# Conv's last two tap pairs behind the next chunk's rotated q, and turns of the identity at the MLP's borders

## The chip, the cores and the metric

The kernel runs on one core of a Trainium2 chip. The metric is the time of one execution on the device, in microseconds (us). Five engines work side by side, each through its own queue in order: TensorE (PE, with its weight loads as PEld), VectorE (DVE), ScalarE (ACT), GpSimd (POOL) and SyncE (SP, which here issues the weight loads from memory). They wait for each other through semaphores.

## The reference

Two blocks run one after the other on x of 256 tokens by 2048 features, float32. The change lies in the first one:

```python
h = rmsnorm(x, norm_mix_pre)
xr, yr, q, k, v, g_rnn, g_attn = split(h @ w_in)
xr = causal_depthwise_conv(xr, conv_w, conv_b)      # 4 taps
xr = rg_lru(xr, ...)
y_rnn = xr * gelu(yr)
q, k = rope(q), rope(k)
y_att = sliding_window_sink_attention(q, k, v, sinks)   # 32 q heads, 4 kv heads, blocks of 128
mix = sigmoid(g_rnn) * (y_rnn @ w_rnn_proj) + sigmoid(g_attn) * (y_att @ w_attn_proj)
x = x + rmsnorm(mix @ w_out)
h = rmsnorm(x, norm_mlp_pre)
x = x + rmsnorm(square(relu(h @ w_mlp_up)) @ w_mlp_down)
```

The second block is a differential attention beside an S5 state space branch, again between a norm and projections.

## The kernel before

**Units and steps.** All large products are cut into units: one unit makes 512 output columns for all 256 tokens from up to 2048 inputs. A unit has 8 steps (4 in the short ones); a step takes one weight tile `raw` of 256 by 512 that SP has loaded. ACT copies it to `w_hi` (rounded to fp32r, L660), DVE subtracts to get `w_lo` (L1149, two inputs in SBUF), and TensorE multiplies the high and low halves of both operands, three matmuls for each block (L1847 to L1850 where the result is laid out by feature, L1855 to L1857 where by token). The four-deep ring lets ACT and DVE run three steps ahead: the function `steps` on each engine splits tile j + 3 and then runs the hooks of place j. Hooks are other work, put between the splits or between the matmuls at places that are written out by hand.

**The stage of q and xr.** First comes a unit for k and v and one for the first 512 columns of q. Then for each of four chunks c a unit of xr and a unit of the next chunk's q follow (three times in a loop; the fourth time the second unit is yr). Beside the two units of chunk c its attention runs, eight heads in four pairs p:

- the rotated q of the chunk, staged in `stg`, is turned (L1870) after the second step of the xr unit; ACT copies it out, and the scores of pair 0 are made (L1926) after the third step, of pair 1 after the fifth
- `soft(p)` on DVE scales the scores and adds the mask (L1326, which frees the score bank for the next pair), then takes the maxima; for pair 0 it stands behind the fourth `w_lo` of the unit
- ACT's exponentials (L775 to L778), DVE's totals (L1338, L1339), and POOL's `normalise` (L499, two instructions)
- TensorE turns the probabilities (L1937), ACT copies them (L784), and TensorE multiplies by v (L1944)

At the end of the q unit DVE's `rotate_q` reads the product and writes the rotated q to `stg`, four instructions for each half of the tokens: two that read PSUM (L1279, L1280) and two that read `tmp` and `tmp2` in SBUF (L1282, L1283). The last one counts up `stg_ready`, for which the turn of the next chunk waits. DVE then goes on with the next three `w_lo`.

**POOL in this stage** has one queue: for each chunk the normalising of pairs 0 and 1, the first tap of conv (L513), the normalising of pairs 2 and 3, and then three pairs of conv instructions, each a multiply to `tap` (L518) and an add (L520) over 4 x 256 elements in each partition. `conv(c, 0)` counts up `conv_ready`, for which DVE waits before it writes the next chunk's xr over conv's input.

**The borders of the MLP.** Before the MLP and behind it, x gets a normed residual. TensorE has ended its last unit; ACT sums squares, DVE forms the mean square, POOL takes the root, and DVE's `residual(c)` (L1517) writes the new x, quarter by quarter. `turn_x(c)` (L1885) waits for each quarter (`x_new`) and turns it in two halves; ACT's `x_high` (L708) and DVE's `x_low` (L1198) copy it out to `h_hi` and `h_lo`; the first unit behind the border begins when quarter 0 is copied. The banks `side[0]` and `side[1]` take the odd quarters. No wait of another engine stands on `side[1]` between the last unit and the first turn into it.

Of the kernel before, what the change touches and what calls it, by code (L numbers as in the profile page):

```python
# [16 lines left out]
P = 128  # L17
# [15 lines left out]
NH = D // NC  # L33
# [61 lines left out]
def griffin_block_then_ssm_block(nc, a, inv_freq, out):  # L95
    with ExitStack() as ctx:
        def sb(name, shape, dt=F32):
            return ctx.enter_context(nc.sbuf_tensor(name, shape, dt))
# [10 lines left out]
        def sem(name):  # L109
            return ctx.enter_context(nc.semaphore(name))  # L110
# [19 lines left out]
        ident = sb("ident", [P, P])  # L130
# [32 lines left out]
        side = [sides[:, n * NC:(n + 1) * NC] for n in range(2)]  # L163
# [9 lines left out]
        stg_ready, tps_ready, tps_hi = sem("stg_ready"), sem("tps_ready"), sem("tps_hi")  # L173
# [102 lines left out]
        T_K, T_QX = NH, NH + 1  # L276
# [54 lines left out]
        def lin(i, stride, const):  # L331
            return const if i is None else i * stride + const
# [101 lines left out]
        def _(pool):  # L434
# [47 lines left out]
            for n in range(5):  # L482
                pool.wait_ge(ms_ready, n + 1)
                pool.tensor_tensor(small[:, 6:8], small[:, 4:6], neg_half[:, 0:2], ALU.pow).then_inc(rstd_ready, 1)
                if n == 0:

                    def load_rg(c):
                        for g, name in enumerate(("w_rg_a", "w_rg_x")):
                            for b in range(2):
                                pool.dma_start(rgw[c % 2][g][:, 2 * b:2 * b + 2, :],  # L490
                                               a[name][0][2 * c + b].rearrange("(k p) c -> p k c", p=P))\
                                    .then_inc(rgw_landed[c % 2], 16)

                    def normalise(i, c, p):

                        pool.wait_ge(total_ready, lin(i, 4, 4 * c + p + 1))
                        for t, at in ((0, slice(0, P)), (1, slice(P, 3 * P))):
                            r_ = att[:, 2 * p:2 * p + 2, 10 + t:11 + t].broadcast_to([P, 2, at.stop - at.start])
                            ins = pool.tensor_tensor(prob[p][:, :, at], prob[p][:, :, at], r_, ALU.mult)  # L499
                            if t == 0:  # L500
                                chain.mark(ins)
                        ins.then_inc(norm_ready, 1)

                    def conv(c, k):


                        late = 3 - k
                        if k == 3:
                            for m in range(QPC):
                                at = c * QPC + m  # L510
                                w = pt1[:, COL1["conv_w"] + KT * k + at:COL1["conv_w"] + KT * k + at + 1]
                                b = pt1[:, COL1["conv_b"] + at:COL1["conv_b"] + at + 1]
                                chain.mark(pool.tensor_scalar(slab_d[:, at, :], xr_c[:, m, :], w, b, ALU.mult, ALU.add))  # L513
                            chain.wait()
                            return
                        at = COL1["conv_w"] + KT * k + c * QPC
                        w = pt1[:, at:at + QPC].unsqueeze(2).broadcast_to([P, QPC, SEQ - late])
                        chain.link(pool.tensor_tensor(tap[:, :, late:], xr_c[:, :, 0:SEQ - late], w, ALU.mult))  # L518
                        o = slab_d[:, c * QPC:(c + 1) * QPC, late:]
                        ins = pool.tensor_tensor(o, o, tap[:, :, late:], ALU.add)  # L520
                        if k:
                            chain.link(ins)
                        else:
                            ins.then_inc(conv_ready, 1)

                    load_rg(0)
                    pool.wait_ge(tps_ready, NH)
                    load_rg(1)

                    pool.sem_inc(conv_ready, 1)  # L530
                    for c in range(NH):
                        normalise(None, c, 0)
                        normalise(None, c, 1)
                        pool.wait_ge(acc_free[0], c + 2)
                        conv(c, 3)
                        normalise(None, c, 2)
                        normalise(None, c, 3)
                        conv(c, 2)
                        conv(c, 1)
                        conv(c, 0)  # L540
                    for c in range(2, NH):
                        pool.wait_ge(rg_done, c - 1)
                        load_rg(c)
                    pool.wait_ge(pe_used, U_OUT * S)
                    pool.dma_start(slab_i[:, :, :].rearrange("p (t k) c -> p t (k c)", t=TT),
                                   a["x"][0].rearrange("(t p) d -> p t d", p=P)).then_inc(post_landed, 16)
                    pool.dma_start(slab_f[:, 0:8, :].rearrange("p k c -> p (k c)"),
                                   a["norm_mix_post"].broadcast_to([P, D])).then_inc(post_landed, 16)
                    pool.dma_start(slab_f[:, 8:16, :].rearrange("p k c -> p (k c)"),
                                   a["norm_mlp_post"].broadcast_to([P, D])).then_inc(post_landed, 16)  # L550
                    for n_, name in enumerate(("ssm_b_re_2", "ssm_b_im_2")):
                        pool.dma_start(b_raw[:, n_], a[name][0].rearrange("(t h) p c -> (h p) t c", h=2)).then_inc(b_landed, 16)
                    for n_, name in enumerate(("ssm_c_re_2", "ssm_c_im_2")):
                        pool.dma_start(c_raw[:, n_], a[name][0].rearrange("(m g) c p -> (g c) m p", g=8)).then_inc(b_landed, 16)
                    chain.link(pool.iota(keep[:, 1, :].bitcast(I32), [[1, SEQ]], base=0, channel_multiplier=0))
                    pool.tensor_copy(keep[:, 0, :], keep[:, 1, :].bitcast(I32)).then_inc(t_ready, 1)
# [55 lines left out]
        def x_bank(c, b):  # L612

            if c % 2 == 0:
                return tps[:, b * SEQ:(b + 1) * SEQ]
            return side[b // 2][:, b % 2 * SEQ:(b % 2 + 1) * SEQ]

        SCORES_AT = [5, 9, 15, 19]
        SOFT_AT = [k // 2 + 1 for k in SCORES_AT]
        TURN_P_AT = [13, 18, 23, 28]
# [1200 lines left out]
        def _(pe):  # L1824
            T = nc.tensor
# [37 lines left out]
            def turn(i, stride, t_index, blocks=QPC):  # L1863
# [7 lines left out]
                                          ident[:, :])  # L1871
                ins.then_inc(tps_ready, 1)

            def turn_x(c, t0, first_x):

                if first_x is None:
                    pe.wait_ge(x_landed[c], 16)
                else:
                    pe.wait_ge(x_new, first_x + c + 1)
                if t0 or c >= 2:  # L1880
                    pe.wait_ge(tps_free, t0 + max(c - 1, 0))
                for half, done in enumerate((x_half, tps_ready)):
                    for t in range(TT):
                        for b in (2 * half, 2 * half + 1):
                            ins = T.transpose(x_bank(c, b)[:, t * P:(t + 1) * P],  # L1885
                                              x_tok[:, t, c * NC + b * P:c * NC + (b + 1) * P], ident[:, :])
                    ins.then_inc(done, 1)
# [23 lines left out]
            for c in range(2):  # L1911
                turn_x(c, 0, None)
# [4 lines left out]
            def attention(i, c):  # L1917
# [12 lines left out]
                def turn_p(p):  # L1930
                    pe.wait_ge(norm_ready, lin(i, 4, 4 * c + p + 1))
                    if p:
                        pe.wait_ge(att_out, lin(i, 4, 4 * c + p))
                    for n in range(2):
                        for b in range(3):
                            at = slice(b * P, (b + 1) * P)
                            ins = T.transpose(turned_p[:, n, at], prob[p][:, n, at], ident[:, :])  # L1937
                    ins.then_inc(pt_done, 1)
# [10 lines left out]
                for p, at in enumerate(SOFT_AT):  # L1949
                    places += [(SCORES_AT[p], lambda p=p: scores(p)), (TURN_P_AT[p], lambda p=p: turn_p(p)),  # L1950
                               (TURN_P_AT[p] + 2, lambda p=p: by_v(p))]
# [46 lines left out]
            for c in range(NH):  # L1998

                unit(None, 0, (U_OUT + c) * S, 0, U_OUT + c, slab_dr, slab_gr,  # L2000
                     hooks={5: [lambda: turn(None, 0, T_MIX + NH - 1)]} if c == 0 else None,
                     before={6: [lambda: pe.wait_ge(tps_free, T_MIX + NH)]} if c == 0 else None)
            for c in range(2):
                turn_x(c, T_MLP_IN, 0)

# [10 lines left out]
            with pe.Fori(0, NH - 1) as f:  # L2016
                mlp_units(f, 1)

            for c in range(2):
                turn_x(c, T_N2, NH)  # L2020

# [166 lines left out]
```

## Time and profile before

| | |
|---|---|
| Median of 3 runs | 2317.41 us (2316.6 to 2319.15) |
| The profiled execution | 2315.3 us |
| Its span, first to last instruction | 2313.6 us |
| Mean granted TensorE clock | 0.996 of full |
| PE busy | 2252.5 us |
| DVE, ACT, POOL busy | 1429.7, 1197.5, 383.3 us |

An engine's busy time is the time covered by its instructions; an instruction that another one holds up in memory counts as busy for as long as it takes. The time that an engine sits idle shows in a timeline in square brackets, with the engine and line that released it. A timeline merges like instructions that follow each other into one row: the first number is its start, the second the time from the start of the first to the end of the last, and xN says how many they are.

### The profile page before, as it was taken

The numbers are of one execution on the slowest core, as the hardware profiler recorded it, in microseconds if no ns is written. First come the engines' busy times: TensorE is split into PE (matmuls) and PEld (weight loads), VectorE is DVE, ScalarE is ACT, GpSimd is POOL, SyncE is SP. The second block draws the span as 40 slices with busy tenths as digits, with TensorE's granted clock in tenths as the row PEclk, the third lists the DMA queues.
The fourth block names the chain that finished last, engine by engine and source line by source line (L and its number), as shares of the span: only waits on it lengthen the run. The fifth ranks groups of instructions, "written<-read, shape, count | busy, mean of one in ns | idle before, by whom it ended". The sixth has DMA issues, their size and how long they took to land.

```text
span 2313.6 us, 32956 instructions
## 1 busy us (share of the span) xinstructions
PE 2252.5 (97%) x11754; PEld 1893.6 (82%) x11754; DVE 1429.7 (62%) x1625; ACT 1197.5 (52%) x1851; POOL 383.3 (17%) x408
## 2 busy tenths in 40 slices
PE   7999999999999999999999999998999999999999
PEld 6888899788888778888888888888977778888887
DVE  6666657644554575555555555566799977675554
ACT  5555557544444446555555555555444445554442
POOL 2133440000000102212122121211243311110000
PEclk9999999999999999999999999999999999999999
DMA  8544454566666846666666666665566655556655
GB/s 246 166 140 138 140 151 149 174 190 192 190 190 193 262 157 199 201 204 205 196 204 201 194 208 201 197 206 171 178 177 182 186 172 170 164 164 188 187 189 163
DMA packets 215027, 427.01 MB, mean 185 GB/s; under 512 B 14032, under 2 KB 14320, under 8 KB 214384
## 3 DMA queue, kind: packets, MB, share of 16 engines
q1 hardware_dynamic: 206720, 398.51, 56.3%
q0 software_dynamic: 7744, 26.62, 3.6%
q8 instruction: 83, 1.36, 0.2%
q14 instruction: 48, 0.39, 0.0%
q10 hardware_dynamic: 432, 0.13, 0.0%
HBM read 414.71 MB, written 10.49 MB: 184 GB/s over the span
## 4 chain that ended last, share of the span: by engine, by line
PE 82%; DVE 9%; ACT 3%; issue 3%; DMA 2%; POOL 1%; SPq 0%; ACTq 0%; DVEq 0%
PE acc L1855 23%; PE acc L1857 23%; PE acc L1856 22%; PE acc L1847 3%; PE acc L1849 3%; PE acc L1850 3%; DVE w_lo L1149 3%; PE tps L1870 1%; DMA raw<-in_w_out_dram 1%; ACT w_hi L660 1%; DMA raw<-in_w_in_dram 1%; PE tps L1976 1%; PE sides L1976 1%; PE sides L1926 1%; POOL tmp L577 1%
## 5 line engine op out<-in xcount | busy, mean ns | idle before, releaser
L1149 DVE TENSOR_TENSOR w_lo<-raw,w_hi 128x1024 fp32r<-128x1024 f32 x752 | 938.7, 1252 | 769.1 <-ACT w_hi L660 764.4
L660 ACT ACTIVATE w_hi<-raw 128x1024 fp32r<-128x1024 f32 x752 | 794.4, 1059 | 905.6 <-PE acc L1857 746.1
L1855 PE MATMUL acc<-w_hi,h_hi 128*128 128x512 f32 x1440 | 572.8, 398 | 6.9 <-DVE w_lo L1149 5.8
L1857 PE MATMUL acc<-w_hi,h_lo 128*128 128x512 f32 x1440 | 562.8, 391 | 0.0
L1856 PE MATMUL acc<-w_lo,h_hi 128*128 128x512 f32 x1440 | 561.9, 390 | 0.0
L1855 PEld LDWEIGHTS acc<-w_hi,h_hi 128*128 128x128 f32 x1440 | 271.2, 188 | 75.0 <-issue 15.8
L1857 PEld LDWEIGHTS acc<-w_hi,h_lo 128*128 128x128 f32 x1440 | 271.0, 188 | 57.8
L1856 PEld LDWEIGHTS acc<-w_lo,h_hi 128*128 128x128 f32 x1440 | 271.4, 188 | 53.2
L1855 PE MATMUL acc<-w_hi,slab_dg_r 128*128 128x512 f32 x768 | 300.1, 391 | 3.9 <-DVE w_lo L1149 3.9
L1857 PE MATMUL acc<-w_hi,slab_dg_r 128*128 128x512 f32 x768 | 299.3, 390 | 0.0
L1856 PE MATMUL acc<-w_lo,slab_dg_r 128*128 128x512 f32 x768 | 299.3, 390 | 0.0
L1847 PE MATMUL acc<-h_hi,w_hi 128*128 128x256 f32 x768 | 222.0, 289 | 3.1 <-DVE w_lo L1149 2.8
L1849 PE MATMUL acc<-h_lo,w_hi 128*128 128x256 f32 x768 | 217.9, 284 | 0.0
L1850 PE MATMUL acc<-h_hi,w_lo 128*128 128x256 f32 x768 | 217.8, 284 | 0.0
L1855 PEld LDWEIGHTS acc<-w_hi,slab_dg_r 128*128 128x128 f32 x768 | 144.6, 188 | 34.2 <-issue 4.3
L1857 PEld LDWEIGHTS acc<-w_hi,slab_dg_r 128*128 128x128 f32 x768 | 144.4, 188 | 30.0
L1856 PEld LDWEIGHTS acc<-w_lo,slab_dg_r 128*128 128x128 f32 x768 | 144.6, 188 | 29.8
L1847 PEld LDWEIGHTS acc<-h_hi,w_hi 128*128 128x128 f32 x768 | 147.5, 192 | 9.7 <-issue 5.8
L1849 PEld LDWEIGHTS acc<-h_lo,w_hi 128*128 128x128 f32 x768 | 147.7, 192 | 0.2
L1850 PEld LDWEIGHTS acc<-h_hi,w_lo 128*128 128x128 f32 x768 | 147.7, 192 | 0.0
L1855 PE MATMUL acc<-w_hi,slab_f_r 128*128 128x512 f32 x256 | 100.4, 392 | 0.0
L1857 PE MATMUL acc<-w_hi,slab_h_r 128*128 128x512 f32 x256 | 99.7, 389 | 0.0
(371 smaller groups left out, 2315.1 us busy)
## 6 DMA issues: line engine op xcount, KB each, us to landing
raw<-in_w_in_dram SPq DMA_DIRECT2D x328, 512.0 KB, 3.8
raw<-in_w_mlp_up_dram SPq DMA_DIRECT2D x128, 512.0 KB, 3.8
raw<-in_w_mlp_down_dram SPq DMA_DIRECT2D x128, 512.0 KB, 4.7
raw<-in_w_out_dram SPq DMA_DIRECT2D x64, 512.0 KB, 4.6
raw<-in_w_rnn_proj_dram SPq DMA_DIRECT2D x32, 512.0 KB, 4.4
raw<-in_w_attn_proj_dram SPq DMA_DIRECT2D x32, 512.0 KB, 3.9
trig_scratch<-tmp POOLq DMA_DIRECT2D x32, 256.0 KB, 4.3
raw<-in_w_proj_ssm_dram SPq DMA_DIRECT2D x16, 512.0 KB, 3.8
```

The costliest lines, as they stand in the source:

```text
L577: pool.tensor_tensor(t1[:, 0, :], t1[:, 0, :], t2[:, 1, :], ALU.add).then_inc(mixed_ready, 1)
L660: nc.scalar.activation(w_hi[:, j % RING], raw[:, j % RING], ACT.Copy).then_inc(hi_ready, 1)
L1149: V.tensor_tensor(w_lo[:, j % RING], raw[:, j % RING], w_hi[:, j % RING].bitcast(F32), ALU.subtract)\
L1847: T.matmul(o, wh[:, c], hi[:, k, :], start=first and m % 2 == 0, stop=False, skip_group_check=True)
L1849: T.matmul(o, wh[:, c], lo[:, k, :], start=False, stop=False, skip_group_check=True)
L1850: ins = T.matmul(o, wl[:, c], hi[:, k, :], start=False, stop=last, skip_group_check=True)
L1855: T.matmul(o, hi[:, k, c], wh, start=first, stop=False)
L1856: T.matmul(o, hi[:, k, c], wl, start=False, stop=False)
L1857: ins = T.matmul(o, lo[:, k, c], wh, start=False, stop=last)
L1870: ins = T.transpose(tps[:, b * SEQ + t * P:b * SEQ + (t + 1) * P], stg[:, t, b * P:(b + 1) * P], ident[:, :])
L1926: ins = T.matmul(side[n][:, t * P:t * P + (t + 1) * P], q_c[at, p, t * P:(t + 1) * P], k_c[at, 0:(t + 1) * P], start=True, stop=True)
L1976: ins = T.matmul(bank[:, m * SEQ:(m + 1) * SEQ], rgw[c % 2][g][:, 2 * b + k, m * P:(m + 1) * P], slab_d[:, c * QPC + 2 * b + k, :], start= ...
```

## The change

In POOL's queue a wait is put between the second and the third tap of conv, for chunks 0 to 2: the last two multiply and add pairs, four instructions, begin only when DVE has announced the rotated q of the next chunk. On TensorE a function `keep_turning` is added that transposes the identity into the four quarters of `side[1]`, which nobody reads; it is called 32 times ahead of the first `turn_x` before the MLP and 44 times ahead of the first behind it.

```diff
                         conv(c, 2)
+                        if c < NH - 1:
+                            pool.wait_ge(stg_ready, T_QX + c + 2)
                         conv(c, 1)
                         conv(c, 0)
...
+        WARM = [32, 44]
...
+            def keep_turning(times):
+
+                for n in range(times):
+                    T.transpose(side[1][:, n % 4 * P:(n % 4 + 1) * P], ident[:, :], ident[:, :])
...
+            keep_turning(WARM[0])
             for c in range(2):
                 turn_x(c, T_MLP_IN, 0)
...
             with pe.Fori(0, NH - 1) as f:
                 mlp_units(f, 1)
 
+            keep_turning(WARM[1])
             for c in range(2):
                 turn_x(c, T_N2, NH)
```

## Rows read from the trace of the kernel before

**Rows 1.** The page: busy time and share of the span, each engine.

```profile
PE 2252.5 (97%) x11754; PEld 1893.6 (82%) x11754; DVE 1429.7 (62%) x1625; ACT 1197.5 (52%) x1851; POOL 383.3 (17%) x408
```

**Rows 2.** Timeline of PE, stage of q: start, duration, what, idle before.

```profile
130.32 1.09 PE L1870 MATMUL tps<-ident,stg 128*128 128x128 f32 x8 [2.47 <-DVE stg L1283]
...
141.01 0.93 PE L1926 MATMUL sides<-k_c,slab_dg_f 64*128 64x128 f32 x8
...
147.73 0.81 PE L1937 MATMUL tps<-ident,slab_i_f 128*128 128x128 f32 x6
...
151.35 0.88 PE L1944 MATMUL tps<-slab_e_f,pi 128*64 128x128 f32 x12
...
189.61 1.09 PE L1870 MATMUL tps<-ident,stg 128*128 128x128 f32 x8 [2.47 <-DVE stg L1283]
...
250.30 1.09 PE L1870 MATMUL tps<-ident,stg 128*128 128x128 f32 x8 [2.39 <-DVE stg L1283]
```

**Rows 3.** Timeline of DVE: rotation without conv (66.89), and a chunk later.

```profile
66.89 0.42 DVE L1282 TENSOR_TENSOR stg<-tmp 128x256 f32<-128x256 f32 x1
...
116.07 1.43 DVE L1149 TENSOR_TENSOR w_lo<-raw,w_hi 128x1024 fp32r<-128x1024 f32 x1 [2.06 <-ACT w_hi L660]
...
123.45 1.90 DVE L1282 TENSOR_TENSOR stg<-tmp 128x256 f32<-128x256 f32 x1
125.27 2.10 DVE L1283 TENSOR_TENSOR stg<-tmp 128x256 f32<-128x256 f32 x1
...
128.60 1.25 DVE L1282 TENSOR_TENSOR stg<-tmp 128x256 f32<-128x256 f32 x1
...
130.87 3.50 DVE L1149 TENSOR_TENSOR w_lo<-raw,w_hi 128x1024 fp32r<-128x1024 f32 x3 [0.68 <-DVE stg L1283]
...
136.55 0.95 DVE L1326 SCALAR_TENSOR_TENSOR slab_i_f<-sides,mask 128x768 f32<-128x768 f32 x1
```

**Rows 4.** Timeline of POOL, the same chunk.

```profile
114.54 1.89 POOL L518 TENSOR_TENSOR slab_e_f<-slab_dg_f,pt 128x1020 f32<-128x1020 f32 x1
...
122.67 2.39 POOL L520 TENSOR_TENSOR slab_dg_f<-slab_dg_f,slab_e_f 128x1016 f32<-128x1016 f32 x1
125.14 1.94 POOL L518 TENSOR_TENSOR slab_e_f<-slab_dg_f,pt 128x1012 f32<-128x1012 f32 x1
...
144.00 1.62 POOL L499 TENSOR_TENSOR slab_i_f<-slab_i_f,att 128x256 f32<-128x256 f32 x2 [14.43 <-DVE att L1339]
```

**Rows 5.** Timeline of DVE, a place in the S5 stage.

```profile
1711.05 1.58 DVE L1149 TENSOR_TENSOR w_lo<-raw,w_hi 128x1024 fp32r<-128x1024 f32 x1
1712.55 1.23 DVE L1640 TENSOR_TENSOR_SCAN k_t<-s5p,k_t 128x256 f32<-128x256 f32 x1
```

**Rows 6.** Timeline of POOL at the same place.

```profile
1711.51 1.73 POOL L578 TENSOR_TENSOR k_t<-k_t 128x256 f32<-128x256 f32 x1
```

**Rows 7.** Timeline of ACT: the first exponential of pair 0, the copy L784.

```profile
139.21 0.28 ACT L775 ACTIVATE att<-att,sinks 128x2 f32<-128x2 f32 x1
...
149.40 0.79 ACT L784 ACTIVATE slab_e_f<-tps 128x768 f32<-128x768 f32 x1
```

**Rows 8.** Windows of 1 us: length, busy each engine, clock, DMA.

```profile
192.00:193.00 1.00, 1.00 (x7) 1.00 (x6) 1.00 (x2) 0.36 (x1) 0.00 (x0) 0.50 0.60 59
...
859.00:860.00 1.00, 1.00 (x6) 0.85 (x5) 1.00 (x4) 0.99 (x4) 0.00 (x0) 0.50 0.00 0
860.00:861.00 1.00, 0.77 (x5) 0.50 (x4) 1.00 (x3) 1.00 (x4) 0.00 (x0) 0.99 0.03 8
```

**Rows 9.** Timeline of PE at the borders: first turns of x.

```profile
856.58 1.97 PE L1885 MATMUL tps<-ident,slab_i_f 128*128 128x128 f32 x8 [4.30 <-DVE slab_i_f L1517]
...
863.29 1.04 PE L1885 MATMUL tps<-ident,slab_i_f 128*128 128x128 f32 x8
...
1580.41 1.97 PE L1885 MATMUL tps<-ident,slab_i_f 128*128 128x128 f32 x8 [5.47 <-DVE slab_i_f L1517]
```

**Rows 10.** Timeline of DVE at the first border: `x_low` of quarter 0.

```profile
858.61 1.73 DVE L1198 SCALAR_TENSOR_TENSOR h_lo<-tps,pt,h_hi 128x256 fp32r<-128x256 f32 x4 [0.76 <-ACT h_hi L708]
```

## The prediction

> **What bounds the kernel now.** I read the page first: TensorE is busy for 97% of the span [rows 1], so time comes only out of its idle stretches, of its clock, or out of new idle put into it. The view of waits over the whole span then names who ends its idle time; two entries belong to this change, the turn of the rotated q (L1870) and the first turn of x at the two borders of the MLP (L1885). The timelines give their places. Three turns of the rotated q find TensorE idle for 2.47, 2.47 and 2.39 us [rows 2], 7.33 us in all; the borders find it idle for 4.30 and 5.47 us [rows 9].
>
> **Why the rotated q is late.** Rotating one chunk takes VectorE eight instructions. In the chunk without conv beside it, the one that reads two SBUF tiles and writes half of stg takes 0.42 us; one chunk later its like take 1.90, 2.10 and 1.25 us [rows 3]. Put against the POOL rows [rows 4] these are waits: the one issued at 123.45 ends 0.29 us after conv's add ends (122.67 + 2.39 = 125.06), the one issued at 125.27 ends 0.29 us after conv's next multiply (125.14 + 1.94 = 127.08). So an instruction of VectorE with two SBUF inputs isn't slowed in proportion, it is held until the running POOL instruction ends. The w_lo subtraction behaves alike: issued at 116.07, it ends at 117.50, 1.07 us after the multiply issued at 114.54 ends at 116.43. The holding goes in turns. In the later S5 stage w_lo is issued at 1711.05, a POOL add at 1711.51, and VectorE's scan at 1712.55, when w_lo is all but done; the POOL add ends first (1713.24) and the scan only at 1713.78 [rows 5, 6]. VectorE doesn't keep the access because its next instruction stands ready: whoever asked first has it. The Trainium skill says that GpSimd shares its SBUF interfaces with VectorE and collides with instructions of two SBUF inputs (GPSIMD Engine Reference, Key points). The rows agree, and add the turns. By the page alone, conv beside w_lo would be no cheaper than conv beside the rotation.
>
> **Part 1, removed.** Conv's last four POOL instructions leave the rotation. Its end moves from 130.19 (0.13 before the turn at 130.32) by 1.48 + 1.68 + 0.83 = 3.99 us to 126.2. TensorE comes to the turn at 130.32 - 2.47 = 127.85, 1.65 us later. The three waits, 7.33 us, go.
>
> The clock comes with it. After the second turn TensorE is granted half speed (1.2 of 2.4 GHz) for a few us [rows 8]; the distance from the first turn to the second is 59.29 us and from the second to the third 60.69 us with nearly the same gap in each [rows 2]. That fall cost 1.4 us. It followed one of three equal gaps, so I count it as gone, with 0 and 2.8 as the other ends.
>
> **Part 1, moved.** The four instructions now begin when the rotated q is announced, 126.3. What stands there is w_lo: three subtractions back to back after the rotation (130.87, 3.50 us [rows 3]), then a fourth, then the softmax's first instruction for the next chunk (the scaling at 136.55). VectorE gets to its first w_lo 0.68 us after the rotation (130.87 against 130.19), POOL needs about 0.1 us after a releaser, so POOL goes first, and then they alternate: multiply, w_lo, add, w_lo, multiply, w_lo, add, w_lo. POOL takes 1.89 + 2.39 + 1.89 + 2.39 = 8.56 us, w_lo 4 x 1.07 = 4.28 us: the fourth w_lo ends at 139.1 and the scaling begins at about 139.0. Without any gap and without conv it would begin at 136.55 - 2.47 = 134.1. It is 4.9 us late. The w_lo tiles themselves are in time: the first two end at 129.3 and 132.7, and the two steps that need them lie before the second scores of 138.5, about 3 us each, so they start at about 132.5 and 135.5.
>
> What waits for the scaling, each place as today's row less 2.47 us:
> - The second scores' matmuls (141.01, so 138.54) need the score bank read. It is read at 139.0 + 0.95, seen at 140.05: TensorE waits 1.5 us.
> - The exponentials (ACT, 139.21 [rows 7]) have some 0.3 us to spare now, so they come 4.6 us late. Behind them in ACT's queue stands the next w_hi, behind that w_lo, the totals, and POOL's normalise (144.00, 1.61 us [rows 4]), each right behind the other. Normalise ends at 145.61 - 2.47 + 4.6 = 147.7; TensorE's turn of the probabilities (147.73, so 145.26) goes at 147.8. It is then 2.6 us behind in all.
> - The copy of the turned probabilities (149.40, 0.79 us [rows 7]) ends at 150.19 - 2.47 + 4.6 = 152.3; the product with v (151.35, so 148.88) goes at 152.4: 3.5 us behind in all. After this ACT and VectorE have idle stretches, and I find no further wait in that chunk.
>
> So each of three chunks gives up a wait of 2.4 to 2.5 us and takes up 3.5 us in three smaller ones: 10.5 - 7.33 = +3.2 us. The new wait delays nothing else: POOL's conv ends at about 138, its next work is that normalise, and the copy of xr that overwrites conv's input comes after it. No DMA is moved. The ends: if w_lo were never held, the three new waits would be zero (-7.3); the full holding is the sum above, and waits could grow by 0.3 each if a POOL instruction took longer.
>
> **Part 2, the borders.** 32 and 44 turns of ident into side[1] (unread; its next writer is TensorE itself) are added ahead of the first turn of x. Eight turns at the full clock take 1.04 us [rows 9]: 0.13 us each at most, since the drain of the last one is in it; without it I estimate 0.10. That makes 3.2 to 4.2 us in a gap of 4.30, and 4.4 to 5.7 us in one of 5.47. I take the lower figure, since spacing and not the drain of the last one counts in a row; they are then hidden, the cover being the norm's sums, its root and the residual. At the upper figure the second border loses 0.2 us. What they can give is the clock: the eight turns after the gap take 1.97 us at half speed against 1.04. Only the first four stand before ACT's copy that releases the first h_lo, 0.47 us, and VectorE stood idle for 0.76 us before it [rows 10], so all 0.47 us carries through. Two borders: -0.9 us. The lower end is nothing; the upper end is the clock falling later, on matmuls in place of turns, 1.4 us each.
>
> The Trainium skill has a rule against this part (TensorE: Matmul & The Clock Gate, Part 4): work in transpose mode doesn't count as busy for the clock. The trace disagrees: from 856.58 to 860.2 TensorE ran transposes alone, and the grant went from 0.50 to 0.99 behind them [rows 8]. By that rule the borders would give nothing, and the sum would be 0.9 us higher.
>
> **Sum.** +3.2 - 1.4 - 0.9 = +0.9 us. The profiled execution took 2315.3 us, 1.7 more than its span of 2313.6 and 2.1 less than the median of the three runs, 2317.41. So 2316.2 for such an execution, 2318.3 for the median of runs. A measurement of this kernel can tell about 0.2%, 4.6 us; this is no change.
>
> **Rivals.**
> - *The gap goes and nothing replaces it.* w_lo gets through beside conv at 1.4 us each, as the row at 116.07 has it; then the scaling is no later than 135.5, scores and exponentials are in time, and the whole 7.3 + 1.4 + 0.9 = 9.6 us is gained: 2307.8. For it: w_lo's single instructions beside conv cost little. Against it: those stood alone, with idle time on both sides, and here four stand in a row against four. 22%.
> - *w_lo gets in first.* The alternation begins with VectorE; without the last add in front of it the fourth w_lo ends 2 us sooner, the scaling is 2.9 us late, the second scores don't wait, and behind the exponentials (2.6 us late in place of 4.6) 1.5 us are left of the 3.5: 3 x 1.5 - 7.33 - 1.4 - 0.9 = -5.1, 2312.3. Against it: POOL's 0.1 us against VectorE's 0.68. 12%.
> - *Slower: the clock falls on the scattered waits.* In place of one gap every chunk has waits of 1.5, 1.1 and 0.9 us within 14 us. Today one of three gaps of 2.4 us brought half speed, at 1.4 us. If it fell once in each of three chunks: +0.9 + 3 x 1.4 = +5.1, 2322.5. It decides from the third fall. Against it: each wait is shorter than the gap that brought it once in three. 12%.
> - *The spare turns outlast their gaps.* If they ran at half speed throughout (1.97 us for eight, some 0.22 each), 32 and 44 take 7.0 and 9.7 us, 6.9 us too long. Against it: they follow matmuls at the full clock. Under 3%, within the slower share.
>
> **How the numbers follow.** The forecast has about half, and the rest lies mostly below it. Faster by over 0.2% (under 2312.8) takes the first rival and a good half of the second: 0.29. Slower by over 0.2% (over 2322.0): 0.13. Within: 0.58. The range goes from the first rival to the third, 2307.8 to 2322.5; the likeliest case alone would be 2316 to 2321.
>
> **What would show it.** In the changed profile the three waits of L1870 for stg are gone, and the rotation takes 4.1 us in each chunk. TensorE's waits have new entries: scores (L1926) for the scaling (L1326), turns (L1937) for normalise (L499) and the product with v (L1944) for ACT's copy (L784), three of each and some 10 us together. The w_lo rows behind the rotation read 2.4 to 3.6 us. At the borders the grant stays at full, x's first eight turns take about 1.1 us, and the unit starts 0.5 us sooner. If w_lo there reads 1.4 us and L1926 doesn't wait, the first rival holds. The prediction is wrong if the turns at the port aren't kept, or if POOL starts later than I think.

## The result, and the profile after

The changed kernel takes 2326.0 us (median of 13 runs, 2319.05 to 2330.54), the kernel before 2317.22 us (13 runs beside them, 2316.09 to 2319.19). The ratio is 1.0033, 95% interval 1.0024 to 1.0041: slower by a third of a per cent. The prediction said 2318.3 with a range up to 2322.5, and gave slower 13%. The time lies outside the range.

The profiled execution of the changed kernel has a span of 2324.3 us at a granted clock of 0.994; before it was 2313.6. I cut both spans at five places that both have, all on TensorE: the first turn of the rotated q; the first by-feature matmul behind the conv stage (330.18 before); the end of the last matmul ahead of the first border; the MLP's first unit; and the first turn of x at the second border.

| stretch | before, us | after, us | difference |
|---|---|---|---|
| start to first turn of the rotated q | 71.12 | 71.45 | +0.33 |
| to the first by-feature matmul (conv stage) | 259.06 | 259.82 | +0.76 |
| to the first border's gap | 522.10 | 521.19 | -0.91 |
| border to the MLP's first unit | 8.16 | 7.63 | -0.53 |
| MLP's first unit to the first turn at the second border | 719.97 | 728.50 | +8.53 |
| the rest | 733.20 | 735.71 | +2.51 |

The two stretches that the prediction argued about, conv and first border, came out at +0.2 us together. The -0.91 us between them can't be put down to the change: there TensorE's longest wait for a `w_lo` was 3.9 us before and 2.9 here, and it lies between 2.9 and 3.9 in the other profiled kernels too, in those that share a part of the change and in those that don't. The loss is in the MLP, where the change alters no instruction. Each of these lengths is that of one execution of each kernel; the 13 runs of the changed one spread over 11.5 us, so its pauses may differ from run to run.

The waits of TensorE in the changed kernel (engine, tile, line waited for: us in total, times, longest):

```profile
PE acc L1858 <- issue: 8.5, 5, 4.5
...
PE sides L1934 <- DVE slab_i_f L1329: 4.0, 3, 1.3
...
PE tps L1945 <- POOL slab_i_f L499: 3.0, 3, 1.1
...
PE tps L1952 <- ACT slab_e_f L787: 2.2, 3, 0.8
PE tps L1893 <- DVE slab_i_f L1520: 1.5, 2, 0.8
```

The turn of the rotated q waits for stg nowhere, where before it had 7.3 us in three. The three new entries of three waits each are the ones forecast. The first turns of x at the two borders wait 1.5 us together in place of 9.8. And one entry that nobody forecast: 8.5 us in which a matmul of the units waited for nothing but its own engine ("issue"); before, the same entry was 1.2 us in two. The first of the five, 0.91 us at 860.09, lies ahead of the loop, at the border; the other four lie inside it. The five in TensorE's timeline:

```profile
860.09 0.47 PE L1858 MATMUL acc<-w_hi,h_hi 128*128 128x512 f32 x1 [0.91 <-issue]
...
1218.01 0.49 PE L1858 MATMUL acc<-w_hi,h_hi 128*128 128x512 f32 x1 [0.41 <-issue]
...
1220.82 0.40 PE L1858 MATMUL acc<-w_hi,h_hi 128*128 128x512 f32 x1 [1.85 <-issue]
...
1397.64 0.39 PE L1860 MATMUL acc<-w_hi,slab_dg_r 128*128 128x512 f32 x1
1398.83 0.49 PE L1858 MATMUL acc<-w_hi,h_hi 128*128 128x512 f32 x1 [0.81 <-issue]
1399.16 0.40 PE L1859 MATMUL acc<-w_lo,h_hi 128*128 128x512 f32 x1
1399.39 0.39 PE L1860 MATMUL acc<-w_hi,h_lo 128*128 128x512 f32 x1
1404.27 0.59 PE L1858 MATMUL acc<-w_hi,h_hi 128*128 128x512 f32 x1 [4.48 <-issue]
1404.65 0.63 PE L1859 MATMUL acc<-w_lo,h_hi 128*128 128x512 f32 x1
```

The input of the matmuls changes from slab_dg_r to h_hi at 1218.01 and at 1398.83. Those are the two places where the loop over f jumps back to its top (three iterations of some 180 us each, behind the unrolled first eight units). At each, TensorE pauses at the jump, does three matmuls, and pauses again, for 1.85 us and for 4.48 us. Before, the first jump had one pause and the second none that is put down to issue (a step of 0.42 us); the usual step from one matmul to the next is 0.23 us:

```profile
1217.58 0.39 PE L1857 MATMUL acc<-w_hi,slab_dg_r 128*128 128x512 f32 x1
1218.89 0.49 PE L1855 MATMUL acc<-w_hi,h_hi 128*128 128x512 f32 x1 [0.92 <-issue]
1219.22 0.40 PE L1856 MATMUL acc<-w_lo,h_hi 128*128 128x512 f32 x1
...
1396.51 0.39 PE L1857 MATMUL acc<-w_hi,slab_dg_r 128*128 128x512 f32 x1
1396.93 0.49 PE L1855 MATMUL acc<-w_hi,h_hi 128*128 128x512 f32 x1
1397.27 0.39 PE L1856 MATMUL acc<-w_lo,h_hi 128*128 128x512 f32 x1
```

Behind the long pause the matmuls last 0.63 us and stand 0.43 apart in place of 0.23. The windows (length, busy and count of PE, PEld, DVE, ACT, POOL, granted clock, DMA share, GB/s) show why:

```profile
1400.00:1401.00 1.00, 0.00 (x0) 0.00 (x0) 0.06 (x1) 0.91 (x1) 0.00 (x0) 0.96 0.88 324
1401.00:1402.00 1.00, 0.00 (x0) 0.00 (x0) 1.00 (x1) 0.00 (x0) 0.00 (x0) 0.50 0.78 301
...
1406.00:1407.00 1.00, 1.00 (x4) 0.81 (x3) 0.00 (x0) 0.00 (x0) 0.00 (x0) 0.50 0.05 16
```

The grant fell to half, 1.2 GHz, while TensorE stood, and stayed there through the first eight matmuls. The idle time in the loop is 7.6 us (0.41 + 1.85 + 0.81 + 4.48 = 7.55), 6.6 more than before's 0.92; eight matmuls 0.2 us further apart are 1.6 us more. That makes 8.2 of the 8.53 us.

### The profile page after: what moved, and what is told of

Same layout as the page of the kernel before. It is cut to its first block, busy times and chain, and to the rows that moved or that the text cites. A ratio compares the mean times of both kernels' runs of the same rounds, so it can differ in the third digit from the quotient of the medians.

```text
span 2324.3 us, 33111 instructions
## 1 busy us (share of the span) xinstructions
PE 2265.3 (97%) x11830; PEld 1902.7 (82%) x11830; DVE 1439.9 (62%) x1625; ACT 1196.6 (51%) x1851; POOL 389.6 (17%) x408
## 4 chain that ended last, share of the span: by engine, by line
PE 79%; DVE 11%; ACT 4%; issue 3%; DMA 2%; POOL 1%; SPq 0%; DVEq 0%; ACTq 0%
PE acc L1858 23%; PE acc L1860 22%; PE acc L1859 22%; DVE w_lo L1152 4%; PE acc L1850 2%; PE acc L1853 2%; PE acc L1852 2%; ACT w_hi L663 1%; PE tps L1873 1%; DMA raw<-in_w_out_dram 1%; DMA raw<-in_w_in_dram 1%; POOL k_t L579 1%; POOL tmp L579 1%; PE tps L1984 1%; PE sides L1984 1%
## 5 line engine op out<-in xcount | busy, mean ns | idle before, releaser
L1152 DVE TENSOR_TENSOR w_lo<-raw,w_hi 128x1024 fp32r<-128x1024 f32 x752 | 961.7, 1283 | 769.1 <-ACT w_hi L663 764.6
L1858 PE MATMUL acc<-w_hi,h_hi 128*128 128x512 f32 x1440 | 575.1, 399 | 12.9 <-issue 8.5
```

The source lines that it names most:

```text
L1152: V.tensor_tensor(w_lo[:, j % RING], raw[:, j % RING], w_hi[:, j % RING].bitcast(F32), ALU.subtract)\
L1858: T.matmul(o, hi[:, k, c], wh, start=first, stop=False)
```

## The experiments

Each ratio is to the kernel before, run on the same chip beside it, with its 95% interval. The kernels are told in the order in which they divide the question.

**Conv alone: e1_conv_only.** The added wait of POOL stays, no turns.

```diff
-        WARM = [32, 44]
+        WARM = [0, 0]
```

> Conv's late tap pairs alone, no spare turns. Theory A (the loss lies in TensorE's instruction supply at the MLP loop, brought by the 32 turns that stand ahead of it in the code): the loop's back edges look as before, with idle time by issue of 1 us or less in all, and the time is that of before within 3 us (three gaps of 2.4 us gone, waits of 3.2 us in their place in each chunk, the clock's fall of 1.4 us perhaps gone). Theory B (the loss comes with conv's shift, since everything after it lies at other times against the DMA traffic): idle time by issue of 5 us or more at the MLP loop, and about +8 us.

Measured: 2317.68 us, ratio 0.9997 (0.9988 to 1.0005). The three new waits are 4.0, 3.0 and 2.2 us in total, as in the changed kernel. The conv stage takes 259.81 us, 0.75 more than before, and the MLP stage 719.28. Conv's part costs next to nothing, and it doesn't touch the loop.

**Turns alone: e2_turns_only.** The added wait is taken out again, both sets of turns stay.

```diff
-                        if c < NH - 1:
-                            pool.wait_ge(stg_ready, T_QX + c + 2)
```

> The turns at both borders alone, conv as before. Theory A: idle time by issue of 4 to 8 us at the MLP loop's back edges, a clock fall behind the longest, +5 to +9 us. Theory B: no such idle time, and -1 us from the borders. The three waits for the rotated q of 2.4 us are back.

Measured: 2324.13 us, 1.0031 (1.0022 to 1.0041). The whole loss comes with the turns. The MLP stage takes 727.37 us:

```profile
1220.35 0.39 PE L1856 MATMUL acc<-w_hi,h_hi 128*128 128x512 f32 x1 [2.29 <-issue]
...
1402.35 0.53 PE L1856 MATMUL acc<-w_hi,h_hi 128*128 128x512 f32 x1 [2.02 <-issue]
```

The pauses stand at the same two jumps, again behind three matmuls, with other lengths. Behind both of them seven or eight matmuls last 0.63 us, which is half clock as behind the 4.48 us above; behind the changed kernel's 1.85 us none did.

**The second border's turns alone: e3_second_only.** These 44 turns stand behind the loop in the program, the other 32 ahead of it.

```diff
-        WARM = [32, 44]
+        WARM = [0, 44]
```

(and without POOL's added wait)

> Only the 44 turns behind the MLP loop. They stand behind the loop in the code, so by theory A the loop is as before and the time is before's less 0.4 us. A rival C, that any added code on TensorE costs (program length, not place), gives +4 us or more here too.

Measured: 2316.1 us, 0.9994 (0.9985 to 1.0003); MLP stage 719.28 us, and no entry for issue inside it. The 44 turns behind the loop leave it alone, so it is the 32 that matter. They could matter because they run (TensorE comes to the MLP with no rest and a full clock) or because they stand in the code ahead of the loop. The next kernels part the two.

**The same 32 turns, 850 us earlier: e4_turns_at_start.** They run at the kernel's start, where TensorE has nothing to do; the borders have none, and POOL's added wait is out.

```diff
+            keep_turning(32)
...
-        WARM = [32, 44]
+        WARM = [0, 0]
```

> 32 turns of the identity at the kernel's start, where TensorE sits idle for 9.6 us until x lands, none at the borders; they move all later code of TensorE by as much as the border's 32 do. Theory A in its narrow form (what counts is where the loop's code lies): the MLP loop shows idle time by issue of 4 to 8 us and the time is +5 to +9 us, though nothing is added near the MLP. Rival D (it is the running of the turns at the border, just before the loop, that upsets the supply): the MLP loop is as before, and the time too, within 2 us.

Measured: 2324.39 us, 1.0033 (1.002 to 1.0046). The first border is now as before (first eight turns 1.95 us behind a gap of 4.30), and the loop still pauses; the MLP stage takes 725.52 us:

```profile
1221.71 0.50 PE L1857 MATMUL acc<-w_lo,h_hi 128*128 128x512 f32 x1 [1.79 <-issue]
...
1403.57 0.50 PE L1857 MATMUL acc<-w_lo,h_hi 128*128 128x512 f32 x1 [1.84 <-issue]
```

At both jumps the long pause now comes behind four matmuls, in place of three; behind the first of them eight matmuls run at half clock. The turns don't have to run near the loop. It is enough that they stand somewhere ahead of it.

**The same turns at the borders, in less code: e5_rolled.** Each set is a hardware loop over four turns, eight times and eleven times.

```diff
-                for n in range(times):
-                    T.transpose(side[1][:, n % 4 * P:(n % 4 + 1) * P], ident[:, :], ident[:, :])
+                with pe.Fori(0, times // 4):
+                    for n in range(4):
+                        T.transpose(side[1][:, n * P:(n + 1) * P], ident[:, :], ident[:, :])
```

(and without POOL's added wait)

> The turns at both borders, 8 and 11 times a loop of four in place of 32 and 44 written out; conv as before. The code ahead of the MLP loop grows by 4 turns and a loop in place of 32. Theory A (place of the loop's code): the MLP loop's idle time by issue differs from that with 32 written out (5.7 us in five places); if it is 1.5 us or less, the borders' gain shows, -1 us against before. Rival D (running turns before the loop upsets it): still 4 us or more. A small loop may lose time at each of its own back edges; if that makes the turns outlast the gap, the first turn of x starts later than 857.

Measured: 2314.58 us, 0.9986 (0.9977 to 0.9995); MLP stage 719.50 us. The turns run as in the changed kernel, the borders look the same (gap 0.80, first eight turns 1.09), and the loss is gone.

**Is it the amount of code, or the place that it gives the loop? e8_64_at_start and e11_16_at_start.** As e4_turns_at_start, with 64 and with 16 turns.

```diff
-            keep_turning(32)
+            keep_turning(64)
```

> 64 turns of the identity at the start, conv as before. They take about 12 us at half speed against TensorE's idle 9.6, so up to 5 us are lost there, which the start of the first unit shows. The question is the MLP loop: if its stall depends on the loop's place in a repeating way, twice the shift can bring the idle time by issue back to 1 us; if it grows with all that is added ahead, it is above 6 us; if any shift from the present place costs the same, 3 to 6 us.

> 16 turns at the start, conv and borders as before: a third place between 0 and 32. If the place counts by small units (an instruction or a few), anything from 0 to 8 us. If 0 and 64 are good and 32 is bad by a period of 64, the middle one shows whether the bad place is narrow (no stall, 719 to 720 us for the MLP stage) or wide (4 us or more).

Measured: with 64, 2315.22 us, 0.9991 (0.9982 to 1.0), MLP stage 718.43; with 16, 2317.41 us, 0.9999 (0.999 to 1.0008), MLP stage 719.80 with one pause of 0.3 us. The start lost less than was expected: with 64 the first turn of the rotated q comes at 71.92 us, before at 71.12. With 64 the jumps can't be seen any more, the matmul behind each follows at the usual step:

```profile
1218.02 0.39 PE L1858 MATMUL acc<-w_hi,slab_dg_r 128*128 128x512 f32 x1
1218.24 0.39 PE L1856 MATMUL acc<-w_hi,h_hi 128*128 128x512 f32 x1
...
1395.73 0.39 PE L1858 MATMUL acc<-w_hi,slab_dg_r 128*128 128x512 f32 x1
1395.96 0.39 PE L1856 MATMUL acc<-w_hi,h_hi 128*128 128x512 f32 x1
```

More code isn't worse: 0, 16 and 64 turns' worth are good places, 32 is a bad one.

**The changed kernel with more code still: e10_after_and_32_at_start.** If the place is all that is wrong with the changed kernel, 32 more turns at the start should mend it.

```diff
+            keep_turning(32)
```

> The changed kernel with 32 more turns at the start, in TensorE's idle time: the MLP loop's code lies 64 turns further than before in place of 32. If the stall depends on the place in a repeating way, as the 64 turns at the start without stall suggest, adding code takes the changed kernel's loss away: -6 to -9 us against the changed kernel, 2317 to 2319, and the MLP stage from the first unit to the border's turn takes 719 us in place of 728. If the 32 turns at the border cost by being there, the loss stays.

Measured: 2313.57 us (11 runs, 2311.8 to 2315.57), 0.9979 (0.997 to 0.9988), with a span of 2313.6 in its profile. The MLP stage takes 718.44 us without a pause inside it. By adding work to the changed kernel it becomes 12 us faster (2326.0 to 2313.57, two medians that weren't taken beside each other), and faster than before by 0.21%, 2.8 to 7 us. Part of this gain over before comes with the place that 64 turns give the loop: e8_64_at_start, with neither part of the change, has 0 to 4.2 us, and the same MLP stage. So what the change itself does, conv and borders, shows no loss, and how much of the gain is its own isn't shown. What its code does to the loop's place costs more than that. The time lies below the 2317 to 2319 that were expected.

Eight kernels and the two of the case in one table, each MLP stage from one execution; "ahead" is what stands ahead of the loop in TensorE's program beyond the kernel before:

| kernel | ahead | MLP stage, us | ratio |
|---|---|---|---|
| before | nothing | 719.97 | 1 |
| e1_conv_only | nothing | 719.28 | 0.9997 |
| e3_second_only | nothing | 719.28 | 0.9994 |
| e5_rolled | a loop of 4 turns | 719.50 | 0.9986 |
| e11_16_at_start | 16 turns | 719.80 | 0.9999 |
| e4_turns_at_start | 32 turns | 725.52 | 1.0033 |
| e2_turns_only | 32 turns | 727.37 | 1.0031 |
| after | 32 turns | 728.50 | 1.0033 |
| e8_64_at_start | 64 turns | 718.43 | 0.9991 |
| e10_after_and_32_at_start | 64 turns | 718.44 | 0.9979 |

**Conv's last pair behind the next normalise: e6_last_pair_later.** The forecast's other half was that conv's four instructions must be held against something. The last two of them are moved behind the next chunk's first normalise; no turns, no added wait.

```diff
                         normalise(None, c, 0)
+                        if c:
+                            conv(c - 1, 0)
...
-                        if c < NH - 1:
-                            pool.wait_ge(stg_ready, T_QX + c + 2)
                         conv(c, 1)
-                        conv(c, 0)
+                    conv(NH - 1, 0)
```

> No turns. The third tap pair stays where it was before the change, ahead of the rotation's end; the last pair of a chunk goes behind the next chunk's first normalise. By the taking of turns at the port: one of the rotation's instructions is held once, by 1.5 us, so the rotated q is ready within 0.1 us of TensorE's coming; no POOL instruction of conv stands beside the four w_lo, so the scores, the turned probabilities and the product with v don't wait. The three waits of 2.4 us go and nothing replaces them: -7 to -8.5 us. If the loss of the late pairs had another cause than the four w_lo beside them (POOL's work in that chunk at all), waits of 3 us a chunk stay and the time is that of before.

Measured: 2307.75 us, 0.9959 (0.9946 to 0.9973). VectorE's timeline in the same chunk:

```profile
123.10 1.90 DVE L1285 TENSOR_TENSOR stg<-tmp 128x256 f32<-128x256 f32 x1
...
128.01 3.50 DVE L1152 TENSOR_TENSOR w_lo<-raw,w_hi 128x1024 fp32r<-128x1024 f32 x3 [0.68 <-DVE stg L1286]
...
133.70 0.95 DVE L1329 SCALAR_TENSOR_TENSOR slab_i_f<-sides,mask 128x768 f32<-128x768 f32 x1
...
143.28 2.85 DVE L1152 TENSOR_TENSOR w_lo<-raw,w_hi 128x1024 fp32r<-128x1024 f32 x1
```

One instruction of the rotation is still held, and the turn of the rotated q doesn't wait; three w_lo run free in 3.50 us; the scaling begins at 133.70, where before it was 136.55 [rows 3] and in the changed kernel 139.03. The pair that was moved holds a w_lo at 143.28 for 2.85 us and the next one, at 146.67, for 2.80, and TensorE waits for neither. Of all three chunks TensorE waits 0.4 us.

**One pair waits, one doesn't: e12_one_pair_waits.** The changed kernel's wait, one line further down; no turns.

```diff
-                        if c < NH - 1:
-                            pool.wait_ge(stg_ready, T_QX + c + 2)
                         conv(c, 1)
+                        if c < NH - 1:
+                            pool.wait_ge(stg_ready, T_QX + c + 2)
                         conv(c, 0)
```

> No turns; the wait for the rotated q stands ahead of the last tap pair alone, so the third pair is back beside the rotation. By the turns at the port: the rotation is held once (by about 1.5 us) and the rotated q is ready within 0.2 us of TensorE's coming; two of the four w_lo are held in place of four, the scaling starts 2.3 us late, the scores don't wait, and about 1 us of waits is left in a chunk (0.9 of it at the product with v): -4 to -5.5 us. If holding were in proportion to time side by side, and not by whole instructions, the wait for the rotated q would be about 1.2 us in each chunk.

Measured: 2310.25 us, 0.9963 (0.995 to 0.9977).

```profile
129.13 8.37 DVE L1152 TENSOR_TENSOR w_lo<-raw,w_hi 128x1024 fp32r<-128x1024 f32 x4 [0.68 <-DVE stg L1286]
...
137.42 0.94 DVE L1329 SCALAR_TENSOR_TENSOR slab_i_f<-sides,mask 128x768 f32<-128x768 f32 x1
```

Two POOL instructions hold four w_lo to 8.37 us in place of 11.90. Neither the scores nor the rotated q wait; what is left are 2.1 us for ACT's copy (0.82 at most in a chunk) and 0.2 for normalise. TensorE's busy time between 120 and 180 us, for before, the changed kernel, this one and e6_last_pair_later in turn:

```profile
120.00:180.00 60.00, 57.53 (x411) 49.45 (x408) 40.52 (x54) 31.18 (x68) 24.95 (x19) 1.00 0.47 144
```

```profile
120.00:180.00 60.00, 56.78 (x401) 48.84 (x400) 43.15 (x54) 31.03 (x67) 26.66 (x19) 1.00 0.48 139
```

```profile
120.00:180.00 60.00, 58.95 (x418) 50.21 (x417) 42.68 (x54) 31.84 (x69) 27.78 (x20) 1.00 0.50 148
```

```profile
120.00:180.00 60.00, 60.00 (x424) 51.79 (x421) 42.78 (x58) 32.55 (x69) 29.04 (x20) 1.00 0.49 148
```

POOL's conv instructions are the same in all four kernels; what differs is how many of them stand against work that somebody waits for.

**The best parts together: e7_later_and_44 and e9_later_rolled_44.** e6_last_pair_later with the second border's 44 turns; then the first border's 32 as well, as a loop of four.

```diff
-            keep_turning(WARM[0])
+            with pe.Fori(0, 8):
+                keep_turning(4)
```

> As the kernel with the last pair later, and the 44 turns behind the MLP loop, whose code moves nothing in that loop. By theory A the two add up: -7.5 to -9.5 us, the fastest of all. If code added anywhere costs, it is slower than the one without turns by 3 us or more.

> The last conv pair behind the next chunk's first normalise, the first border's 32 turns as 8 times a loop of four, the second border's 44 written out. By the place of the code: no stall of over 1 us at the MLP loop, and the first border's 0.4 us on top of the kernel with 44 turns alone: -10 to -13 us against before, ratio about 0.995. If the small loop's code moves the MLP loop to a bad place, 5 us or more of this are lost.

Measured: 2305.3 us, 0.995 (0.9936 to 0.9963), and 2304.89 us, 0.9942 (0.9928 to 0.9955). The last is 12.9 us below the 2317.76 of before beside it, and 21 us below the changed kernel's median. Its loop has no long pause: MLP stage 719.22 us. The intervals of e6, e7 and e9 overlap, so what the turns add to e6 isn't shown; their common gain over the kernel before and the changed one is.

## Why the prediction was wrong

**The step that failed** is in Part 2: 32 and 44 turns "are then hidden, the cover being the norm's sums, its root and the residual". I priced an added instruction by the time for which it runs, and found cover for that. The cover was there, and the 32 turns were counted as costing nothing. But an instruction also takes room in the program, and everything behind it moves. The change puts 32 instructions ahead of the MLP's loop on TensorE, and in its new place that loop's jumps cost 6.6 us of idle time and 1.6 us of half clock. The sum had no term for it, no rival named it, and the 0.92 us of "issue" at the first jump was in the profile before: it showed that the jumps cost something, and that one did so more than the other. These 8.2 us are most of the 10.7 between the two profiled executions. Neither slower rival happened: the clock didn't fall on the scattered waits of the conv stage (the windows from 120 to 240 us show a grant of 1.00 in the changed kernel), and the spare turns didn't outlast their gaps (below).

That the turns' place, and not their running, is the cause is shown: the same 32 turns cost the same 850 us earlier (1.0033 against 1.0031), cost nothing as a loop, and 32 more of them undo it. What the place does is not shown. That TensorE's supply of instructions comes late after a jump to some addresses is how I read "issue" at the jumps; no view shows the supply. Open too are why the second pause comes a few matmuls behind the jump, at a fixed place in each kernel (behind three matmuls at both jumps of the changed kernel and of e2_turns_only, behind four at both of e4_turns_at_start), why its length varies from 1.79 to 4.48 us between the profiled executions, and where between 16 and 64 the bad places begin and end.

**Conv, the removed part: right.** The rotation runs free, its instructions back at 0.43 and 0.42 us, and the turn waits for nothing. The 7.33 us are gone, and so is the half clock behind the second turn. How many such falls the three gaps bring differs between executions: one in the profile of the kernel before, two in those of e3_second_only and e4_turns_at_start, with conv as before (a mean grant of 0.97 from 120 to 180 and from 180 to 240 us), none in the changed kernel's.

**Conv, the moved part: the mechanism right, the size 1.3 us too high.** VectorE and POOL in the changed kernel:

```profile
123.77 0.43 DVE L1285 TENSOR_TENSOR stg<-tmp 128x256 f32<-128x256 f32 x1
...
127.20 11.90 DVE L1152 TENSOR_TENSOR w_lo<-raw,w_hi 128x1024 fp32r<-128x1024 f32 x4 [0.68 <-DVE stg L1286]
...
139.03 0.95 DVE L1329 SCALAR_TENSOR_TENSOR slab_i_f<-sides,mask 128x768 f32<-128x768 f32 x1
```

```profile
126.67 1.88 POOL L518 TENSOR_TENSOR slab_e_f<-slab_dg_f,pt 128x1016 f32<-128x1016 f32 x1 [6.57 <-DVE stg L1286]
128.63 3.24 POOL L520 TENSOR_TENSOR slab_dg_f<-slab_dg_f,slab_e_f 128x1016 f32<-128x1016 f32 x1
```

POOL starts first and the four w_lo take 11.90 us: the full holding, with the scaling at 139.03 where 139.0 was forecast. One by one they take 2.43, 3.40, 2.89 and 3.41 us, and each ends 1.08 or 1.09 us after the POOL instruction beside it: the turns as forecast. POOL is held in turn (3.24 us for an add of 2.39). The waits are

```profile
140.03 0.93 PE L1934 MATMUL sides<-k_c,slab_dg_f 64*128 64x128 f32 x8 [1.32 <-DVE slab_i_f L1329]
...
147.97 0.88 PE L1945 MATMUL tps<-ident,slab_i_f 128*128 128x128 f32 x6 [1.08 <-POOL slab_i_f L499]
...
152.54 0.88 PE L1952 MATMUL tps<-slab_e_f,pi 128*64 128x128 f32 x12 [0.82 <-ACT slab_e_f L787]
```

1.32, 1.08 and 0.82 us against 1.5, 1.1 and 0.9, so 9.2 us in nine against 10.5. With the 7.33 that is +1.9 us where the sum had +3.2; with the clock's 1.4 it would be +0.5, and the stage took 0.76 us longer (0.75 in e1_conv_only). Both rivals on the faster side, w_lo beside conv at 1.4 us each and w_lo getting in first, are out: the row of 11.90 us decides against both.

**The borders: right as far as they go.** The turns take 3.66 us for 32 and 4.97 us for 44, within the two bounds given, and the grant stays full:

```profile
852.30 3.66 PE L1880 MATMUL sides<-ident 128*128 128x128 f32 x32
...
856.76 1.09 PE L1893 MATMUL tps<-ident,slab_i_f 128*128 128x128 f32 x8 [0.81 <-DVE slab_i_f L1520]
...
1582.94 4.97 PE L1880 MATMUL sides<-ident 128*128 128x128 f32 x44
...
1588.59 1.09 PE L1893 MATMUL tps<-ident,slab_i_f 128*128 128x128 f32 x8 [0.68 <-DVE slab_i_f L1520]
```

```profile
857.00:858.00 1.00, 0.85 (x8) 0.62 (x6) 1.00 (x2) 0.54 (x2) 0.00 (x0) 1.00 0.00 0
...
859.00:860.00 1.00, 0.18 (x2) 0.00 (x0) 1.00 (x4) 1.00 (x5) 0.00 (x0) 1.00 0.00 0
...
1591.00:1592.00 1.00, 0.09 (x2) 0.12 (x2) 1.00 (x4) 1.00 (x4) 0.00 (x0) 1.00 0.00 0
```

Eight turns take 1.09 us where they took 1.97 [rows 9], and the unit follows them 0.5 us sooner (3.33 us from the first turn of x to the unit, before 3.86). From the end of the last matmul to the first turn of x it is 4.30 us in both kernels, so the turns don't delay it and the whole 0.53 us carry through; at the second border the unit follows 3.33 us behind the first turn too, before 3.86. The windows answer the rule that transposes don't count as busy for the clock (the Trainium skill, TensorE: Matmul & The Clock Gate, Part 4): at both borders the kernel's transposes alone kept the grant at 1.00 over a gap in which it fell without them, so for these the measurement decides against it. The profile lists them as MATMUL and doesn't show whether the mode that the page speaks of is on. e5_rolled, where the turns are free of the loop's place, gives 0.9986 with an interval from 1.2 to 5.3 us faster; the 0.9 forecast for the borders lies just outside it, and where the rest comes from isn't shown.

**The rest.** The last +2.51 us lie behind the second border, in S5. In the two halves of 1700 to 1800 us the mean grant is 0.93 and 0.93 in the changed kernel against 0.97 and 1.00 before. The first of these falls stands here:

```profile
1718.47 2.08 PE L2058 MATMUL sides<-slab_e_f,pi 32*128 32x256 f32 x8 [2.28 <-DVE k_t L1637]
```

Its like took 1.13 us before, behind the same wait. Such falls appear in some kernels and not in others with the same code there: e10_after_and_32_at_start, with every instruction of the changed kernel, has 0.97 and 1.00. The rest is as long in both other kernels with 32 turns ahead of the loop (735.73 and 736.50 us), but also in e11_16_at_start, whose loop hardly pauses (736.48); in the other profiled kernels it is 732.6 to 734.0. So I put it down to no part of the change, and whether the loop's pauses help to bring it stays open.

## What to carry to other kernels

Added code had two prices here: the time for which it runs, which cover hid, and the shift of all code behind it, which the cover didn't hide. Before adding instructions ahead of a long hardware loop, look for idle time put down to issue at the loop's jumps; after adding them look again, and if it has grown, try the same work as a small loop or with a different amount of code ahead, before you judge the idea. When two engines hold each other at SBUF, moving one's work helps only as far as nobody waits for what it then holds: here four POOL instructions beside a chain that ends in TensorE cost 3.1 us of waits in each chunk, and with two of them beside the rotation and two beside `w_lo` that were early 0.4 us of waits were left in all three chunks.

## What the runs showed of the hardware

- The place of a loop of TensorE in its program is worth up to 8.5 us here: with 0, 16 and 64 instructions' worth of turns added ahead, its two jumps back cost about 1 us or nothing; with 32, 4.2 to 7.6 us of idle time in them. Behind four of the six long pauses (4.48, 2.29, 2.02 and 1.79 us) seven or eight matmuls ran at a grant of 0.50, behind the others (1.85 and 1.84) none. In two of the three kernels with the bad place the runs also scatter more (11.5 and 12.1 us from the fastest to the slowest, against 3.1 to 6.8 of the kernel before); the third has 7.1.
- VectorE and GpSimd alternate at SBUF by whole instructions: four subtractions, of which three take 3.50 us by themselves, took 11.90 us beside four POOL instructions, 8.37 beside two, and POOL's add grew from 2.39 to 3.24 us. Each of the four ended 1.08 or 1.09 us after a POOL instruction.
- Transposes of a constant, with nobody to read them, held TensorE's grant at full over gaps of 4.30 and 5.47 us in which it fell to half without them. They take 0.11 us each.
